# A two-block network on one core: where the moving operands of the matmuls begin in SBUF

## The reference

```
for l in range(2):                       # first block: two layers
    proj = rms_norm(x) @ w_in[l]         # u, z, q, k, v, az, iq, ik, iw, mq, mz, three gates
    y_pool = multi_scale_pool(u) * silu(z)
    y_attn = top-k indexed attention(q, k, v, iq, ik, iw) * silu(az)
    y_mem  = attention(mq, mem_k, mem_v) * silu(mz)
    x = x + (sum over b of sigmoid(g_b) * (y_b @ w_branch[l, b])) @ w_out[l]
x = rms_norm(x)
...
h = [16 meta tokens, x]                  # second block: 272 tokens
q, k, v, z, b, a, sc_b, sc_c, sc_x, gate_a, gate_b = split(rmsnorm(h) @ w_in_2)
o_dn = bidirectional gated delta rule over chunks of 64 tokens
h = h + (sigmoid(gate_a) * (o_dn @ w_dn) + sigmoid(gate_b) * (y_sc @ w_sc)) @ w_out_2
gate, up = split(rmsnorm(h) @ w_gate_up_2)
h = h + (silu(gate) * up) @ w_down_2
return rmsnorm(h)[16:]
```

## Time and profile before

| | |
|---|---|
| median of 3 runs | 1215.74 us (1213.79 to 1220.06) |
| the profiled execution | 1222.06 us, its span 1219.9 us |
| TensorE busy | 1180.0 us, 97% |
| weight loads busy | 1143.1 us, 94% |
| VectorE busy | 850.6 us, 70% |
| ScalarE busy | 618.9 us, 51% |
| granted TensorE clock | 0.99 over the span |

### The profile page before, as it was taken

How to read it: one execution, slowest core, us unless ns; L and a number is a source line. 1 busy time by engine, 2 the same in 40 slices (tenths; PEclk the granted TensorE clock), 3 DMA queues, 4 the chain that set the end, 5 groups by cost and what they waited for, 6 DMA issues and landing times.

```text
span 1219.9 us, 26120 instructions
## 1 busy us (share of the span) xinstructions
PE 1180.0 (97%) x10852; PEld 1143.1 (94%) x10852; DVE 850.6 (70%) x1345; ACT 618.9 (51%) x1012; POOL 223.4 (18%) x250
## 2 busy tenths in 40 slices
PE   6999999999999999999999699999999999999997
PEld 6999999999999999999888699999999999999997
DVE  4855857667868566578699667687785778755554
ACT  6645455544645555536568723333324636544453
POOL 3100150002100520022002016273440051000001
PEclk9999999999999999999999899999999999999999
DMA  8654655455855654456555242333325665666654
GB/s 295 210 176 148 190 173 162 139 150 152 247 154 177 194 163 142 138 157 190 188 158 163 69 136 58 104 96 95 102 70 156 197 206 190 191 188 187 196 192 137
DMA packets 59941, 196.29 MB, mean 161 GB/s; under 512 B 6414, under 2 KB 14120, under 8 KB 59696
## 3 DMA queue, kind: packets, MB, share of 16 engines
q1 hardware_dynamic: 51136, 182.71, 48.8%
q10 hardware_dynamic: 8160, 9.53, 2.4%
q0 software_dynamic: 528, 2.40, 0.8%
HBM read 190.37 MB, written 4.23 MB: 160 GB/s over the span
## 4 chain that ended last, share of the span: by engine, by line
PE 86%; DVE 5%; ACT 3%; issue 2%; DVEq 2%; POOLq 1%; DMA 1%; ACTq 0%
PE stream_ps L310 18%; PE stream_ps L311 18%; PE stream_ps L325 14%; PE stream_ps L304 4%; PE stream_ps L305 4%; PE stream_ps L306 4%; PE free_ps L2304 2%; PE stream_ps L2085 2%; DVE w_lo L296 2%; PE free_ps L2316 2%; PE stream_ps L2398 2%; PE stream_ps L361 1%; PE stream_ps L366 1%; PE stream_ps L362 1%; DVE qkvT L1474 1%
## 5 line engine op out<-in xcount | busy, mean ns | idle before, releaser
L296 DVE TENSOR_TENSOR w_lo<-raw,w_hi 128x1024 fp32r<-128x1024 f32 x342 | 427.8, 1261 | 186.3 <-ACT w_hi L290 184.9
L290 ACT ACTIVATE w_hi<-raw 128x1024 fp32r<-128x1024 f32 x342 | 356.1, 1052 | 60.2 <-PE stream_ps L2085 26.0
L310 PE MATMUL stream_ps<-h_hi,w_hi 128*128 128x256 f32 (+1 forms) x1376 | 336.3, 285 | 2.6 <-DVE h_lo L1803 0.9
L311 PE MATMUL stream_ps<-h_lo,w_hi 128*128 128x256 f32 (+1 forms) x1376 | 329.1, 279 | 0.0
L310 PEld LDWEIGHTS stream_ps<-h_hi,w_hi 128*128 128x128 f32 x1376 | 259.2, 188 | 9.0 <-issue 4.2
L311 PEld LDWEIGHTS stream_ps<-h_lo,w_hi 128*128 128x128 f32 x1376 | 259.5, 189 | 0.5
L325 PE MATMUL stream_ps<-h_hi,w_lo 128*128 128x256 f32 (+1 forms) x1328 | 182.1, 280 | 3.6 <-DVE w_lo L296 3.6
L325 PEld LDWEIGHTS stream_ps<-h_hi,w_lo 128*128 128x128 f32 x1328 | 166.5, 188 | 4.3 <-DVE w_lo L296 4.3
L304 PE MATMUL stream_ps<-h_hi,w_hi 128*128 128x256 f32 (+1 forms) x384 | 117.6, 306 | 7.8 <-DVE w_lo L296 4.3
L305 PE MATMUL stream_ps<-h_lo,w_hi 128*128 128x256 f32 (+1 forms) x384 | 110.2, 287 | 0.0
L306 PE MATMUL stream_ps<-h_hi,w_lo 128*128 128x256 f32 (+1 forms) x384 | 110.2, 287 | 0.0
(11 more groups left out here) (445 smaller groups left out, 2247.6 us busy)
## 6 DMA issues: line engine op xcount, KB each, us to landing
raw<-stream_dram SPq DMA_DIRECT2D x342, 512.0 KB, 3.9
gate_spill<-gate_out ACTq DMA_DIRECT2D x16, 128.0 KB, 2.5
decay<-gate_spill POOLq DMA_DIRECT2D x2, 640.0 KB, 10.9
xT<-xT_dram SPq DMA_DIRECT2D x4, 272.0 KB, 5.3
wik<-wik_dram ACTq DMA_DIRECT2D x2, 544.0 KB, 7.2
mem_raw<-memT_dram SPq DMA_DIRECT2D x2, 512.0 KB, 5.6
hankel<-rel_scratch POOLq DMA_DIRECT2D x1, 1024.0 KB, 8.5
x_spill<-xT ACTq DMA_DIRECT2D x1, 1024.0 KB, 11.6
```

Of the source, the lines that this page charges most:

```text
L290: nc.scalar.activation(w_hi[s][:, :, :], raw[:, s, :].rearrange("p (k n) -> p k n", k=KT), ACT.Copy).then_inc(hi_ready, 1)
L296: nc.vector.tensor_tensor(w_lo[s][:, :, :], raw[:, s, :].rearrange("p (k n) -> p k n", k=KT), w_hi[s][:, :, :].bitcast(F32), ALU.subtract) ...
L310: nc.tensor.matmul(ps, l_hi, r_hi, start=first, stop=False)
L311: nc.tensor.matmul(ps, l_hi, r_lo, start=False, stop=False)
```

## The change

Only places in SBUF change. Every instruction, its order, its shapes and its waits stay as they are; three dummy tiles have other sizes, and four constants other values.

```diff
-LAYER0_AT, LAYER1_AT, OUT_AT, GATE_UP_AT = 112, 112, 112, 112
+LAYER0_AT, LAYER1_AT, OUT_AT, GATE_UP_AT = 120, 104, 116, 116
...
         with ExitStack() as one:
-            sb("home_shift", [P, 112], scope=one)
+            sb("home_shift", [P, 40], scope=one)
...
                 sum_b = sb("sum_b", [P, POOLG, PAD + S], scope=win)
+            sb("y_shift", [P, 16], scope=one)
             mixed = sb("mixed", [P, 2, S], scope=one)
             y_hi = sb("y_hi", [P, 3, 4, S], F32R, one)
...
         with ExitStack() as two:
-            sb("later_shift", [P, 32], scope=two)
+            sb("later_shift", [P, 40], scope=two)
```

## The result

The changed kernel takes 1233.86 us (1232.27 to 1235.08, 3 runs) against 1215.74 us: 1.3% slower, ratio 1.0129, 95% interval 1.0097 to 1.0161. The forecast was 1205 us, so the time moved by 18 us in the other direction.

The account below looks back on a forecast made before the run. TensorE's stream of matmuls was taken as the bound, so time is their number times pitch. The moved matmuls gave -11 us, all else about nothing: 1215.74 - 11 = 1205 us, range 1197 to 1240.

Parts of the forecast that it names:

- The bound: Whole kernel: TensorE, busy 97% of the span, sets the time; new places act only through matmul pitch or few waits.
- B: Other engines and DMAs pay for their shifted tiles; the prediction put this at under 1 us, hidden by TensorE's stream.
- the stable long phase: 256-column stream matmuls: a steady slower way of reading both operands, 117.8 ns each, which shifted starts were to disturb.
- the short level: Faster pitch of 256-column stream matmuls, 113.3 ns (modelled 276), as in layer 0's gates; some 2450 moved matmuls.
- The term of -11 us for the moved matmuls: 6048 moved 256-column matmuls: shifted starts win two thirds of 16 us, a chosen share, not a reading.
- the prize: 16 us paid by some 3600 slower 256-column matmuls, at 4.5 ns each.
- the long level: Slower pitch of 256-column stream matmuls, 117.8 ns (modelled 281), as in gate/up, `y` and the downward product.
- The reading of the earlier trace: Two readings: matmuls with moving weights, starting at 128, show the same levels; `pu`'s unsplit matmuls pay nothing for 32-byte shifts.
- nothing that can be told: Rival, all stages: an interruption sets the level, new starts only redeal or leave it; 1216 us within 6, chance 0.24.
- all long: Rival, moved 256-column matmuls: the faster pitch needs the aligned start, so all run at 117.8 ns; +11 us, chance 0.16.
- The account of the levels: Count by stage of moved 256-column matmuls: some 3600 of 6048 at the slower pitch, including gate/up and downward product.
- The 17th piece: Rival: each moved matmul reads one more 64-byte piece, up to 7.7 ns, 47 us in all, 1262 us; chance 0.14.

Follow-up runs that it names:

- the second of the kernel before: The unchanged kernel run once more with only a comment edited: 1214.95 us in one run, span 1212.9 us against 1219.9.

## Why the prediction was wrong

- *The bound.* Right: TensorE's stream is the bound, its waits did not change, and the whole difference is pitch. B, which was costed at under 1 us, was indeed small.
- *"With the moving operand half or a quarter of a 64-byte piece out of step with the weights at 128 by 512, [...] the stable long phase has less to hold on to."* This is the step that failed. The relative place of the two operands does matter, as this step had it, but the even pitches of 113.3 and 117.8 ns were seen only at distances that are odd multiples of 64, and no stage in which the activations move has a mean under 117 ns at any other distance. Leaving these distances takes away the short level along with the long one and puts mean pitches of 117 to 121 ns in place of both. The term of -11 us for the moved matmuls measured some +14 us (10.9, 1.3, 1.0 and 0.7 us of the sum above). I counted the prize (16 us, what the long level costs) as what a disturbance could win, and what the short level already gave as safe; the runs show the opposite, the change cost the short stages 5 ns a matmul and the long ones 0.5 to 1.4.
- *The reading of the earlier trace rows.* I used it for "nothing that can be told" and against "all long", because the weights as the moving operand begin elsewhere and had the same levels. Their distance is +64, another odd multiple: the row was the same case seen from the other side. It should have pointed at the distance between the two operands rather than at the start of one.
- *The reading of the earlier trace rows.* That a start 32 bytes off costs nothing by itself is true in the split format too (everything moved by 32 bytes, 1.0001). But it says nothing on the distance, which was the matter.
- *The account of the levels.* 3600 long matmuls were read from one execution. Gate/up and the downward product, 1392 of them, are dealt anew from execution to execution, so the prize was nearer 10 us than 16 in an execution such as the second of the kernel before. The mean that the change had to beat was lower in such an execution than I took it to be.
- *The rivals.* "All long", +11 us, came nearest in time (1227 against 1233.86 us) and named the right sign: 276 vanished from the gates of both layers. Its mechanism, that the short way needs the aligned start, is refuted by the run in which everything is moved by 32 bytes. It was 7 us short because most pitches off the levels lie above 117.8 ns. The 17th piece is refuted by the same run. "Nothing that can be told" is refuted by the result and by the gates of both layers; that an interruption sets the level was right, but only between the two levels of a good distance. It also leaned on 16-byte lines, which the Trainium skill, "Advanced Engine Details and Errata", section "SBUF Cachelines", states; all distances of the change were multiples of 16 bytes, and the trace doesn't agree with my reading that this leaves the pitch alone (118.3 to 119.2 ns at -32, -48 and -96).
- *What would show it.* Of the signs of being wrong, the first came true: stages at 276 went to a median of 280. Durations of 285 appeared too, but as the top of an uneven pattern and not as the price of a further piece. The split by stage, 96 against 32 against 80, came out as 118.3, 118.6 and 119.2 ns. All were worse than before, so the difference between them told less than I had hoped, and the runs with one operand moved at a time told more.

Why odd multiples of 64 are good, and what decides which level follows an interruption at one of them, was not found. The table does not fit a pattern that repeats every 128 bytes of distance, for ±128 has 118.6 to 118.7 ns and 0 and 256 have 120.0. It fits one that repeats every 256: -64 behaves as +192, +64 as -192, -128 as +128, 0 as 256 and -32 as +224 (118.3 ns both). That something in SBUF repeats so is only argued.

## What to carry to other kernels

Where TensorE streams full-rate matmuls with a new weight load each, read the pitch by stage from pairs of rows far apart, and tabulate it against the distance between the moving and the stationary operand by 512 bytes, not against either address. Keep that distance at a value that was measured to be good when a tile is added, resized or padded: here a 4-byte slip cost 7.8 ns on 113.3. That another kernel has the same good distances is not shown. And before counting what a stage could win from a second level, profile the same program twice, because the level may be dealt anew.

## What the runs showed of the hardware

- The pitch of a float32r matmul of 256 columns with its own weight load is 113.3 or 117.8 ns at a distance of -64 or +192, 117.8 ns at +64 with the activations moving, and, by stage, 117 to 121 ns at every distance tried that is no odd multiple of 64.
- It depends on the distance, not on the addresses: all tiles moved by 32 bytes gives 1.0001 (0.9973 to 1.0029), the weights alone moved by 32 bytes gives 1.0164 (1.0141 to 1.0188).
- The same program took gate/up and the downward product at 117.8 ns in one profiled execution and at 113.3 in another, 7.0 us of span apart; the two part at one wait of 0.9 us, after which each keeps its level, but for five matmuls, to the end of the downward product.
- At a distance of -96 too a stage has no fixed pitch: the gates of layer 1 had 118.6 ns in the changed kernel and 117.3 ns with only the constants changed.
